# Attention scores of two heads on both row halves, mask and maximum in one operation, and 32-token experts on column quarters

## The reference, cut to what matters

```
def mla_block(qn, qr, kn, kr, v):                       # 6 heads, 96 rows of q and k
    s = (einsum(qn, kn) + einsum(qr, kr)) * MLA_SCALE
    return einsum(softmax(s), v)

# swa_latent: 6 heads of 64 rows, 256 context and 256 local keys
s_loc = where(|q_pos - k_pos| <= 128, einsum(q, k) * SWA_SCALE, -inf)
p = softmax(concat[s_ctx, s_loc, sink])

def ec_ffn(h, router_w, w_gate, w_up, w_down):
    cap = 2 * n_tok // 16                               # 32 tokens for each expert
    top_aff, idx = top_k(softmax(h @ router_w).T, cap)
    xg = h[idx]
    hid = silu(xg @ w_gate) * (xg @ w_up)               # 1024 -> 512
    y = (hid @ w_down) * top_aff                        # 512 -> 1024
    return scatter_add(y, idx)
```

## Time and profile before

| | |
|---|---|
| median of 3 runs | 2282.93 us (2276.14 to 2287.74) |
| profiled execution | 2275.7 us |
| its span | 2273.6 us |
| PE matmuls busy | 2153.0 us, 95% |
| DVE busy | 874.3 us, 38% |
| ACT busy | 455.8 us, 20% |
| HBM traffic | 432.23 MB read |

### The profile page before, as it was taken

The page is one execution under the profiler, slowest core; times in us unless marked ns, Lnnn a source line. Parts: engine busy times, 40 slices in busy tenths (PEclk is TensorE's granted clock), DMA queues, the critical chain, the costliest instruction groups (busy, mean ns, idle before and its releaser), DMA issues.

```text
span 2273.6 us, 29101 instructions
## 1 busy us (share of the span) xinstructions
PE 2153.0 (95%) x12423; PEld 1619.2 (71%) x12423; DVE 874.3 (38%) x1771; ACT 455.8 (20%) x986; POOL 88.7 (4%) x88
## 2 busy tenths in 40 slices
PE   6999999999899999988999999999999998999998
PEld 3444586655555575544878888899888788889997
DVE  2137723132326631112356423466115544146620
ACT  3004523111122420101134112100003321120000
POOL 1000010000000010000001100000000011000000
PEclk9999999999999999999999999999999999999999
DMA  9651504999922359999423314444643231344453
GB/s 370 231 199 42 215 1 185 420 424 420 384 74 81 142 212 409 426 426 411 149 76 110 111 38 148 148 153 141 169 150 124 99 112 42 108 150 172 142 148 94
DMA packets 172913, 435.14 MB, mean 191 GB/s; under 512 B 6218, under 2 KB 64498, under 8 KB 156146
## 3 DMA queue, kind: packets, MB, share of 16 engines
q1 hardware_dynamic: 171648, 430.90, 50.6%
q10 hardware_dynamic: 1138, 2.39, 0.3%
HBM read 432.23 MB, written 1.05 MB: 191 GB/s over the span
## 4 chain that ended last, share of the span: by engine, by line
PE 85%; DMA 7%; DVE 4%; ACT 2%; issue 1%; ACTq 0%; DVEq 0%
PE bank L274 81%; DMA ring<-in_exp_w_up 4%; PE bank L531 2%; PE bank L761 1%; DMA arena<-in_exp_w_up 1%; DMA ring<-in_exp_w_gate 1%; DMA ring<-in_w_in 1%; DMA arena<-in_x 1%; ACT arena L731 0%; DVE arena L726 0%; ACT h L639 0%; ACT h L619 0%; PE bank L1257 0%; PE bank L457 0%; DVE arena L811 0%
## 5 line engine op out<-in xcount | busy, mean ns | idle before, releaser
L274 PE MATMUL bank<-h,ring 128*128 128x256 f32 (+3 forms) x3376 | 750.1, 381 | 12.4 <-ACT arena L585 4.9
L274 PEld LDWEIGHTS bank<-h,ring 128*128 128x128 f32 (+1 forms) x3376 | 594.0, 191 | 153.3 <-issue 77.0
L274 PE MATMUL bank<-arena 128*128 128x128 f32 (+13 forms) x2432 | 392.6, 346 | 27.8 <-issue 9.9
L274 PEld LDWEIGHTS bank<-arena 128*128 128x128 f32 (+5 forms) x2432 | 286.4, 187 | 116.8 <-issue 64.7
L274 PE MATMUL bank<-arena,ring 128*128 128x256 f32 (+1 forms) x1792 | 332.5, 346 | 1.0 <-PE bank L274 1.0
L274 PEld LDWEIGHTS bank<-arena,ring 128*128 128x128 f32 x1792 | 296.0, 191 | 33.0 <-PE bank L274 1.8
L731 ACT ACTIVATE arena<-bank 128x256 f32<-128x256 f32 (+5 forms) x263 | 116.2, 461 | 589.7 <-PE bank L274 564.6
L274 PE MATMUL bank<-ring,arena 128*64 128x256 f32 x1376 | 155.2, 380 | 12.7 <-DMA ring<-in_exp_w_up 7.9
L726 DVE COPY arena<-bank 128x256 f32<-128x256 f32 (+7 forms) x114 | 60.9, 535 | 263.5 <-PE bank L274 211.1
L274 PEld LDWEIGHTS bank<-ring,arena 128*64 128x64 f32 x1376 | 99.0, 137 | 74.7 <-DMA ring<-in_exp_w_up 11.6
L274 PE MATMUL bank<-h,arena 128*128 128x128 f32 (+2 forms) x560 | 106.5, 330 | 4.1 <-ACT arena L1293 2.4
(11 more groups left out here) (319 smaller groups left out, 1647.7 us busy)
## 6 DMA issues: line engine op xcount, KB each, us to landing
ring<-in_w_in SPq DMA_DIRECT2D x31, 2048.0 KB, 7.8
ring<-in_exp_w_gate SPq DMA_DIRECT2D x22, 2048.0 KB, 13.3
ring<-in_exp_w_up SPq DMA_DIRECT2D x21, 2048.0 KB, 13.1
ring<-in_exp_w_down SPq DMA_DIRECT2D x20, 2048.0 KB, 15.3
ring<-in_ada_w SPq DMA_DIRECT2D x18, 2048.0 KB, 10.3
ring<-in_w_ffn_down SPq DMA_DIRECT2D x16, 1408.0 KB, 6.9
ring<-in_w_ffn_gate SPq DMA_DIRECT2D x10, 2048.0 KB, 7.8
ring<-in_w_ffn_up SPq DMA_DIRECT2D x10, 2048.0 KB, 7.8
```

The costliest lines, as they stand in the source:

```text
L274: return PE.matmul(o, lhsT, rhs, start=(k == 0), stop=(k == n - 1))
```

## The change

In `attend_tensor`, the scores of two 64-row heads of the first block are issued in one place, in turn: half 0 of head i, half 0 of head i+1, half 1 of head i, half 1 of head i+1. The four banks are taken ahead of the first matmul. In `attend_vector`, mask and maximum of a half become one `tensor_tensor_reduce` over all key columns; the window's mask table gets 256 more columns of zeros for each query half, and the sign is turned where the maximum is used. Layer 1's modulation results go to bank 7. In the second layer's experts, 32 stationary columns are used, and four matmuls write to the four partition quarters (gate and up: even and odd hidden columns of each half, 128 moving columns each; down: four quarters of the width, 256 each). The two transposes become one, the copies follow, and POOL's clearing goes with its wait.

```
+    near = np.where(np.abs(q - t[None, None, :]) <= 128, 0, NEG)
+    put("window", np.concatenate([near, np.zeros_like(near)], 2).reshape(P, -1), True)
...
-            elif key[0] == "mods_rows":
+            elif key[0] == "mods_rows" or key[0:2] == ("mods", 1):
                 b = 7
...
             def scores(i):
-                q, keys, nk = heads[i][0:3]
+                pair = [i]
+                if heads[i][1].shape[0] == 64 and tag[0] == "heads":
+                    if i % 2:
+                        return
+                    pair = [i, i + 1]
+                taken = {(hd, j): take(pe, "scores", tag, hd, j) for hd in pair for j in range(2)}
                 for j in range(2):
-                    b = take(pe, "scores", tag, i, j)
-                    mm(b[:, 0:nk], q(j), keys, 0, 1).then_inc(*tensor.mark("scores", tag, i, j))
+                    for hd in pair:
+                        q, keys, nk = heads[hd][0:3]
+                        mm(taken[hd, j][:, 0:nk], q(j), keys, 0, 1).then_inc(*tensor.mark("scores", tag, hd, j))
...
                     if mask is not None:
-                        link(dve, V.tensor_tensor(b[:, 0:S], b[:, 0:S], mask[:, j, :], ALU.add))
-                    V.reduce_max(nx[:, j:j + 1], b[:, 0:nk], AX, negate=True).then_inc(*vector.mark("chain"))
+                        V.tensor_tensor_reduce(b[:, 0:nk], b[:, 0:nk], mask[:, j, :], 1.0, LOWEST, ALU.add, ALU.max, nx[:, j:j + 1])\
+                         .then_inc(*vector.mark("chain"))
+                    else:
+                        V.reduce_max(nx[:, j:j + 1], b[:, 0:nk], AX, negate=True).then_inc(*vector.mark("chain"))
...
                     for hf_ in range(2):
-                        last = mm(b[64 * hf_:64 * hf_ + 64, 0:256], xg[:, k, e, :], w[:, k, hf_ * 256:(hf_ + 1) * 256], k, KD)
+                        if NS == 2:
+                            ...
+                            continue
+                        for odd in range(2):
+                            g = 32 * (2 * hf_ + odd)
+                            last = mm(b[g:g + CAP, 0:P], xg[:, k, e, 0:CAP], w[:, k, hf_ * 256 + odd:(hf_ + 1) * 256:2], k, KD)
...
             for f in range(4):
-                for half in range(2):
+                for q in range(4 if NS == 1 else 0):
+                    last = mm(b[32 * q:32 * q + CAP, 0:256], flat_hidT[:, e % 2, f * CAP:(f + 1) * CAP], w[:, f, q * 256:(q + 1) * 256], f, 4)
+                for half in range(2 if NS == 2 else 0):
...
-            if NS == 1:
-                pe.wait_ge(xg_cleared, 1)
...
-                nc.gpsimd.memset(xg[:, :, :, CAP:2 * CAP], 0.0).then_inc(xg_cleared, 1)
```

More of the change, by code:

```diff
@@ L794, in stats @@
                     if mask is not None:
-                        link(dve, V.tensor_tensor(b[:, 0:S], b[:, 0:S], mask[:, j, :], ALU.add))
-                    V.reduce_max(nx[:, j:j + 1], b[:, 0:nk], AX, negate=True).then_inc(*vector.mark("chain"))
+                        V.tensor_tensor_reduce(b[:, 0:nk], b[:, 0:nk], mask[:, j, :], 1.0, LOWEST, ALU.add, ALU.max, nx[:, j:j + 1])\
+                         .then_inc(*vector.mark("chain"))
+                    else:
+                        V.reduce_max(nx[:, j:j + 1], b[:, 0:nk], AX, negate=True).then_inc(*vector.mark("chain"))
                 dve.wait_ge(*vector.now("chain"))
                 nsk = sink.broadcast_to((P, 2))
-                V.scalar_tensor_tensor(nm, nx, scale, nsk, ALU.mult, ALU.min).then_inc(*vector.mark("maxima", tag, i))
+                V.scalar_tensor_tensor(nm, nx, scale if mask is None else -scale, nsk, ALU.mult, ALU.min).then_inc(*vector.mark("maxima", tag, i))
                 dve.wait_ge(*vector.now("maxima"))
@@ L1255, in expert_tensor @@
             b = take(pe, "expert_turned", l, e)
-            for i in range(2):
-                last = PE.transpose(b[:, i * P:(i + 1) * P], hid1[:, e % 2, i:256:2], ident)
+            for i in range(NS):
+                last = PE.transpose(b[:, i * P:(i + 1) * P], hid1[:, e % 2, i:256:2] if NS == 2 else hid1[:, e % 2, 0:P], ident)
             last.then_inc(*tensor.mark("expert_turned", l, e))
@@ L1273, in expert_vector @@
             dve.wait_ge(*tensor.at("expert_up", l, e))
-            V.tensor_tensor(hid1[:, e % 2], hid1[:, e % 2], bank("expert_up", l, e)[:, 0:256], ALU.mult).then_inc(*vector.mark("expert_up", l, e))
+            a = hid1[:, e % 2, 0:P * NS]
+            V.tensor_tensor(a, a, bank("expert_up", l, e)[:, 0:P * NS], ALU.mult).then_inc(*vector.mark("expert_up", l, e))
             between_vector(dve, l, 2 * e)
-            out_vector(dve, hidT[:, e % 2].rearrange("p b n -> p (b n)"), bank("expert_turned", l, e)[:, 0:256], "expert_turned", l, e)
+            out_vector(dve, flat_hidT[:, e % 2, 0:P * NS], bank("expert_turned", l, e)[:, 0:P * NS], "expert_turned", l, e)
             between_vector(dve, l, 2 * e + 1)
@@ L1279, in expert_vector @@
             dve.wait_ge(*tensor.at("expert_down", l, e))
-            for s in range(NS):
-                last = V.tensor_copy(yst[32 * q:32 * q + 32, g % 2, s, 512:1024],
-                                     bank("expert_down", l, e)[64 + s * CAP:64 + (s + 1) * CAP, :])
+            for s in range(2):
+                last = V.tensor_copy(yst[32 * q:32 * q + 32, g % 2, s, 512:1024] if NS == 2 else yst[32 * q:32 * q + 32, g % 2, 0, 512 + 256 * s:768 + 256 * s],
+                                     bank("expert_down", l, e)[64 + s * CAP:64 + (s + 1) * CAP, 0:256 * NS])
             last.then_inc(*vector.mark("expert_down", l, e))
@@ L1286, in expert_scalar @@
             NS = 2 if l < L - 1 else 1
-            out_scalar(act, hid1[:, e % 2], bank("expert_gate", l, e)[:, 0:256], "expert_gate", l, e, func=ACT.Silu)
+            out_scalar(act, hid1[:, e % 2, 0:P * NS], bank("expert_gate", l, e)[:, 0:P * NS], "expert_gate", l, e, func=ACT.Silu)
             between_scalar(act, l, 2 * e)
@@ L1291, in expert_scalar @@
             act.wait_ge(*tensor.at("expert_down", l, e))
-            for s in range(NS):
-                last = SC.activation(yst[32 * q:32 * q + 32, g % 2, s, 0:512], bank("expert_down", l, e)[s * CAP:(s + 1) * CAP, :], ACT.Copy)
+            for s in range(2):
+                last = SC.activation(yst[32 * q:32 * q + 32, g % 2, s, 0:512] if NS == 2 else yst[32 * q:32 * q + 32, g % 2, 0, 256 * s:256 + 256 * s],
+                                     bank("expert_down", l, e)[s * CAP:(s + 1) * CAP, 0:256 * NS], ACT.Copy)
             last.then_inc(*scalar.mark("expert_down", l, e))
```

6 lines of the change are left out of this document (3 added, 3 removed).

## The result

The changed kernel takes 2305.3 us (median of 4 runs, 2298.7 to 2305.8), the kernel before 2280.6 beside it (4 runs, 2276.1 to 2287.7). The ratio is 1.0095, 95% interval [1.0074, 1.0117]: slower by about 1%. The forecast was 2297 with a range of 2270 to 2314.

The account below looks back on a forecast made before the run. PE's program order was taken as the path nearly everywhere, with the second layer's experts waiting for weights by DMA. Attention +16.0, clock +2.8 and experts -4.4 give +14.4 us, from the median 2282.93 to 2297; range 2270 to 2314.

Parts of the forecast that it names:

- The loop: First block's attention: paired scores wait for ACT's exponentials, 11.83 us a pair against 9.60; part 1 sums to +16.0 us.
- Rival B: Attention: PE stays the bound, the loop being shorter than PE's 7.69 us; -18.8 us, 2264; chance 0.11.
- the first pair's wait: Layer 0 attention, heads 6 and 7: four free banks wanted, so a wait for head 5's exponentials, 1.0 us (0 to 2.2).
- The row halves overlap: Paired scores in attention: four matmuls on two row halves take 1.91 us, saving PE 1.91 per pair.
- Rival C: Paired scores: row halves do not overlap, the loop grows by 1.91 us; +12.5 more, 2310; chance 0.08.
- The fused operation: Mask and maximum in one on DVE: 0.79 us with read-out, against 0.42 + 0.69 for the old pair.
- Rival D: Fused mask and maximum on DVE takes two passes: +6 us, 2303; chance 0.08.
- The clock: PE's granted clock in attention: five idles of 2.5 us, two followed by a slow clock, +2.8 us (0 to 7).
- The experts: Second layer's experts on column quarters: PE time mostly hidden behind DMA, early stall and tail shorten, -4.4 us (-5.2 to 0).
- rival F: Second layer's experts: their 88 us of PE lie on the path, 2200; chance 0.01.
- Rival E: Attention: about no change, half of the loop's price found elsewhere; +3 to +6 us, 2287; chance 0.12.

Follow-up runs that it names:

- experiment 3: Changed kernel with matmuls that nobody reads filling TensorE's idle before the score pairs from heads 8 and 9 on: 2294.7 us, ratio 1.0045 to the kernel before.
- experiment 5: Changed kernel with the chunk of modulation rows moved behind the first turning: 2284.4 us, ratio 1.0020 to the kernel before.
- experiment 1: Changed kernel without the pairing of scores, run twice: 2275.1 and 2274.3 us, ratios 0.9958 and 0.9967 to the kernel before.
- experiment 4: Changed kernel with the four score matmuls issued head by head, banks still taken ahead: 2303.3 us, ratio 1.0089 to the kernel before.
- experiment 6: Changed kernel with mask and maximum as two operations again: 2308.7 us, ratio 1.0121 to the kernel before.

## Why the prediction was right, and where it was not

**The loop: right, by mechanism and by size.** PE waits 2.34 us before each pair (about 2.5 forecast), released by ACT's exponential at L848, and 1.57 before the second turning (1.6 forecast). At the full clock a round is 11.8 (experiment 3), forecast 11.83; two of its terms were off by 0.15 and 0.10 and nearly cancel (the two maxima 1.43 for 1.58, the exponentials with PE's start behind them 1.55 for 1.45). Moving one of the loop's terms away took 17 us (experiment 5). Rival B, a pair bound by PE's 7.69, is out. In layer 1, experiment 3, with the clock at 1.00, stands 4.5 above before and 5.8 above experiment 1, in whose trace the last turning has the full clock as well: the forecast term was 5.5. In layer 0 the first pair's wait was 1.6 (1.0 forecast), the third of the three rounds is one head's scores behind the wait and not a pair's (8.55 before, 12.56 in the change, in part by the clock), and from head 10's turning to the end of the context stream experiment 3 took 4.2 more than before (2.8 forecast).

**The row halves overlap: right.** Eight records in 1.99 us at the full clock (experiment 3), and the next group starts 1.91 after them, as forecast. Rival C is out. The price of a pair would be the same with the heads one after the other (experiment 4).

**The fused operation: right.** 0.705 us, and its read-out 0.142. From the start of the first of two to the small operation are 236.03 - 234.60 = 1.43 where 1.58 was taken. Rival D (1.38 each) is out. That it costs or gives nothing outside the loop is shown by 1.0007. The forecast put its worth within the loop in the 11.83 and not in a term of its own; experiment 6 makes it about 7 us. Two halves take 2.25 us there from the first mask to the small operation and 1.43 in the change, 0.8 a loop, so 4.1 in five loops, and the five rounds are 0.3 to 2.1 us longer, 4.7 in all. The rest lies mostly in the context stream. Part is the clock's: in 240 to 254 it was 0.74 without the fused operation and 0.87 with it. The two were not measured apart.

**The clock: the step that failed.** The forecast sum has "two slow ones, +2.8", from one idle that was followed by 4 us at 0.65 and one that was not the earlier trace rows. What it should have asked is what a stretch does that has two idles in every round. The granted clock was under 1 in every window of the paired attention: 0.93, 0.89, 0.87, then 0.50, and 0.85 over 45 us of layer 1, where experiment 3 had 1.00 and before had 0.92 with 18 us behind its attention in the window. At the end of the context stream it varies: the second execution of the change had 1.00 and then 0.62 where the first had 0.80 and 0.50, and before had 0.66 right behind it. The loop's matmuls are on the path, and they took 3.12 and 2.43 us where the full clock gives 1.99 and 1.92. Attention as a whole took 30.5 us more, of which the forecast loops are 16.0, which leaves 14.5; taken directly, the change less experiment 3 is 8.5 to 10.8, a lower bound. So the clock cost some 8.5 to 14.5 us, above the upper bound of 7; the upper end holds only if the loops cost just the forecast 16.0. That bound counted five idles of 2.5 us and left out the ones of 1.6 and those of the context stream.

**The experts: right, in kind and about in size.** -3.4 us from first load to last down between the two profiles, forecast -4.4; over all the traces read, 3 to 5. The period stayed at DMA's 14.7 for three chunks, PE's 88 us were hidden (rival F is out), and the gain is the end: down starts 1.28 us after PE came to wait, at landing, and takes 1.93 instead of 3.65. From the start of the last up to the end of the last down that is 9.21 and 6.91 us, -2.3 where the forecast took -1.7; the other 1.1 are from before that, where it took -2.7. Alone the experts gave 5 to 6 us, and with the fused operation 8 to 9. Of these 3 to 5 are placed in the experts' stage; the rest I can't place, since the profiled execution of before is itself 5 to 7 us under its median.

**The sum.** Over the profile of before: 16.0 + 14.5 - 3.4 = +27.1 against +14.4 forecast. In the measured medians it came out at +22 to +25, inside the range and on the forecast side, 8 us over the predicted value. That the value was this close is in part luck: the terms measured in the profiles, added to the median of before as the forecast did, would have given 2310. Rival E (half of the loop's price) is out.

## What to carry to other kernels

Before taking several PSUM banks at once, count back through the rotation and see who must free the last one: if that is work which the waiting engine itself has still to feed, a full engine becomes a latency loop, and its round is the sum of every step on it, other work queued there included. When such a loop leaves an engine idle in each round, price the clock over the whole stretch and not idle by idle. And if work is to stand beside a wait, put it where the engine idles, not between the wait and the step that the others need.

## What the runs showed of the hardware

- With two idles of 2.34 and 1.57 us in each round of 13.4 us the granted clock was 0.87 to 0.93, where the same stage without them had 1.00. At the end of the context stream, where PE idles 0.6 to 1.5 us at a time, it was 0.80 and then 0.50 for 10 us in one execution, 1.00 and 0.62 in another of the same kernel. With the longer idle filled by matmuls that nobody reads it was 1.00 over 45 us of layer 1. Useless work on PE made a kernel faster by 7 to 11 us (ratios 1.0045 against 1.0095 and 1.0096).
- Four float32 score matmuls on two row halves overlap in either order, in turn or head by head: 2.78 us in both at the same place, 1.99 in both at the full clock.
- Four column quarters of 32 run fully beside each other: 64 records of 128 columns in 2.0 us, 31 ns a record, where one record of the plain scores takes 0.12 us for 128 columns.
- A combined mask and maximum on 512 columns with a mask in SBUF takes 0.705 us, like the plain maximum (0.69), and its read-out 0.14; two of them follow each other in 1.43.
